# A first block opened by halves of the features, with TensorE kept running from the constants on

## The reference

```
mod = silu(c) @ w_ada + b_ada
shift, scale, gate = split(mod, 3)
h = rms_norm(x, norm_g) * (1 + scale) + shift
proj = h @ w_in            # q, six key and value parts, z_a, branch gates, u, z_s
attn = nsa_attention(...) * silu(z_a)
y = s5_mixer(u, ...)       # a complex linear recurrence over the tokens
ssm = gelu(y) * sigmoid(gelu(y) @ glu_w + glu_b) * silu(z_s)
x = x + gate * (concat(attn, ssm) @ w_out)
```

## Time and profile before

| what | value |
| --- | --- |
| median of 3 runs | 906.59 us (906.15 to 906.69) |
| the profiled execution | 905.98 us, span 904.2 us |
| busy share of the span | TensorE 97%, VectorE 64%, ScalarE 50%, GpSimd 11% |
| chain of waits that ended last, by engine | TensorE 92%, VectorE 4%, ScalarE 2%, transfers 1% |
| mean granted clock of TensorE | 0.997 |

### The profile page before, as it was taken

One profiled execution on the slowest core, in us unless ns is written; L12 is line 12 of the kernel. 1 busy time (PEld: TensorE's weight loads), 2 busy tenths in 40 slices (PEclk: granted clock), 3 DMA queues, 4 the chain that ended last, 5 costly groups with the idle time before them and its releaser, 6 DMA issues.

```text
span 904.2 us, 14652 instructions
## 1 busy us (share of the span) xinstructions
PE 875.7 (97%) x5733; PEld 708.0 (78%) x5733; DVE 578.9 (64%) x1154; ACT 450.7 (50%) x956; POOL 99.7 (11%) x121
## 2 busy tenths in 40 slices
PE   3999999999999999999999999999999999999996
PEld 1579888784677778788888888888888888888885
DVE  5899797989888564666465455345476556445533
ACT  4734323386787334465535466234366554555531
POOL 1001112012400000000010232000000001131202
PEclk9999999999999999999999999999999999999998
DMA  9836655347200313323223424122322332342203
GB/s 384 335 98 140 176 159 168 125 133 240 94 2 2 116 62 118 118 88 95 71 94 116 141 94 131 51 94 94 120 88 67 94 106 96 125 140 71 84 10 94
DMA packets 34678, 104.69 MB, mean 116 GB/s; under 512 B 14961, under 2 KB 14961, under 8 KB 32178
## 3 DMA queue, kind: packets, MB, share of 16 engines
q1 hardware_dynamic: 28098, 85.77, 28.5%
q0 software_dynamic: 3856, 15.73, 5.5%
q10 hardware_dynamic: 2656, 2.26, 1.0%
HBM read 98.37 MB, written 4.19 MB: 113 GB/s over the span
## 4 chain that ended last, share of the span: by engine, by line
PE 92%; DVE 4%; ACT 2%; DMA 1%; issue 1%; SPq 0%; POOL 0%; POOLq 0%; ACTq 0%; DVEq 0%
PE bank L1101 85%; PE bank L1461 2%; PE bank L1615 2%; PE bank L1441 2%; DMA ring<-in_w_ada 1%; PE bank L1501 1%; DVE arena L1749 1%; PE bank L1491 0%; ACT arena L768 0%; DVE xn_t L2271 0%; DVE ring_lo L2295 0%; DVE w_lo L2243 0%; ACT soft L861 0%; DVE pw L1743 0%; DVE x_t L2331 0%
## 5 line engine op out<-in xcount | busy, mean ns | idle before, releaser
L2243 DVE TENSOR_TENSOR w_lo<-ring,w_hi 128x1024 fp32r<-128x1024 f32 x80 | 101.4, 1270 | 51.8 <-ACT w_hi L943 49.3
L1101 PE MATMUL bank<-hT_hi,w_hi 128*128 128x512 f32 x320 | 129.4, 404 | 0.0
L1101 PE MATMUL bank<-hT_lo,w_hi 128*128 128x512 f32 x320 | 125.2, 391 | 0.0
L1101 PE MATMUL bank<-hT_hi,w_lo 128*128 128x512 f32 x320 | 124.9, 390 | 0.0
L1101 PE MATMUL bank<-w_hi,hT_hi 128*128 128x512 f32 x256 | 101.7, 397 | 0.3 <-DVE hT_lo L2289 0.3
L1101 PE MATMUL bank<-w_lo,hT_hi 128*128 128x512 f32 x256 | 99.9, 390 | 0.0
L1101 PE MATMUL bank<-w_hi,hT_lo 128*128 128x512 f32 x256 | 99.8, 390 | 0.0
L943 ACT ACTIVATE w_hi<-ring 128x1024 fp32r<-128x1024 f32 x80 | 84.3, 1057 | 14.0 <-PE bank L1101 13.8
L1101 PEld LDWEIGHTS bank<-hT_hi,w_hi 128*128 128x128 f32 x320 | 60.1, 188 | 16.8 <-issue 4.7
L1101 PEld LDWEIGHTS bank<-hT_lo,w_hi 128*128 128x128 f32 x320 | 60.1, 188 | 13.1
L1101 PEld LDWEIGHTS bank<-hT_hi,w_lo 128*128 128x128 f32 x320 | 60.2, 188 | 11.2
(11 more groups left out here) (341 smaller groups left out, 1834.3 us busy)
## 6 DMA issues: line engine op xcount, KB each, us to landing
ring<-in_w_units SPq DMA_DIRECT2D x80, 512.0 KB, 3.7
ring<-in_w_ada SPq DMA_DIRECT2D x4, 2048.0 KB, 10.3
bias_ring<-in_na_bias POOLq DMA_DIRECT2D x6, 1024.0 KB, 5.2
ring<-in_w_out SPq DMA_DIRECT2D x2, 2048.0 KB, 8.8
bias_ring<-in_t_bias POOLq DMA_DIRECT2D x8, 448.0 KB, 3.7
x_t<-in_x SPq DMA_DIRECT2D x4, 512.0 KB, 5.7
arena<-in_w_ada SPq DMA_DIRECT2D x1, 2048.0 KB, 19.9
arena<-in_w_ada SPq DMA_DIRECT2D x2, 1024.0 KB, 22.8
```

The source lines that it names most:

```text
L1101: return pe.matmul(out, lhsT, rhs, start=first, stop=last)
L2243: dve.tensor_tensor(w_lo[:, u % 4], raw_w[:, u % 4], w_hi[:, u % 4].bitcast(fp32), SUB).then_inc(S["w_split"], 1)
```

## The change

The first block's opening is put in a new order. In words:

- SyncE loads chunk 0 into `arena` and chunk 2 into `cl` (a later part of the arena), then the three parts of the u weights, then chunk 1 into ring slot 1. Chunk 3 follows in two parts into the place of chunk 0, behind a wait for the first product with c; tables, rows and the keys' weights stand behind it.
- TensorE makes five fp32 products of the identity and 512 columns of constants into bank 5, whose result nobody reads, as soon as the constants are there.
- The order of the chunks is 0, 2, 1, 3 (`ADA`): shift and scale of the lower half of the features first. `modulate(0)` waits for chunks 0 and 2 alone, `modulate(1)` for 1 and 3.
- Tile 0 of u is made of three passes as the others are, which adds `part_hi(0)` and `part_lo(0)`. All four tiles are made in two halves of four products a pass (`u_pass`): the lower half of the features, with the last two products with c and their columns among the passes, and then the upper half.
- ScalarE's sines for the tables stand behind the rounding of the upper half; before, ahead of all rounding.
- On VectorE the modulation of the lower half stands ahead of the tables, that of the upper half behind their first operations; `part_lo(12)`, `part_lo(13)` and the lambda products stand behind the keys' squares; before, ahead of them.
- The ring's release for the keys' weights is given once, by two, behind the third product with c and the third tile's first half.

```diff
-            for c, parts in enumerate(chunks):
+            sp.dma_start(arena[:, 0:SLOT], ada[0]).then_inc(ada_late_in[0], 16)
+            sp.dma_start(cl[:, 0:SLOT], ada[2]).then_inc(ada_late_in[1], 16)
+            for c in (CH_U, 1, *range(CH_K, len(chunks))):
+                parts = chunks[c]
...
-                if c >= SLOTS:
+                if c > CH_U:
                     sp.wait_ge(S["w_free"], c - SLOTS + 1)
...
-                if c == SLOTS - 1:
-                    sp.dma_start(arena[:, 0:SLOT], ada[2]).then_inc(ada_late_in[0], 16)
+                if c == 1:
+                    sp.wait_ge(S["ada_done"], 1)
                     for n in range(2):
-                        sp.dma_start(arena[:, SLOT + 2048 * n:SLOT + 2048 * (n + 1)], ada[3][:, 2048 * n:2048 * (n + 1)]).then_inc(ada_late_in[1 + n], 16)
-                elif c == CH_U:
+                        sp.dma_start(arena[:, 2048 * n:2048 * (n + 1)], ada[3][:, 2048 * n:2048 * (n + 1)]).then_inc(ada_late_in[2 + n], 16)
...
+            move_rows(0)
+            move_hT(0)
+            move_hT(1)
+            part_hi(0)
+            move_rows(1)
+            move_hT(2)
+            move_hT(3)
+            round_x(0)
+            part_hi(1)
+            part_hi(2)
+            part_hi(3)
+            move_rows(2)
+            move_rows(3)
+            round_x(1)
+            act.wait_ge(S["ang_ready"], 1)
...
+            def u_pass(f, half, which):
+                w, h = ((p_hi, x_hi), (p_lo, x_hi), (p_hi, hT_r))[which]
...
+                for k in range(4 * half, 4 * half + 4):
+                    if f == 0 and which != 1:
+                        pe.wait_ge(S["h_lower" if which else "h_hi"], k + 1)
+                    ins = mm(bank[f][:, :], w(f)[:, k, :], h[:, k, :], which == 0 and k == 0, which == 2 and k == KD - 1)
...
+            for n in range(5):
+                mm(bank[5][:, :], ident, cons[:, 0:512], True, True)
             pe.wait_ge(S["c_silu"], 1)
...
+            pe.wait_ge(ada_late_in[0], 16)
+            times_c(bank[ROW_PLACE[0]], ada_late[0]).then_inc(S["ada_done"], 1)
+            turn_x(0)
+            mod_columns(0)
+            turn_x(1)
+            pe.wait_ge(ada_late_in[1], 16)
+            times_c(bank[ROW_PLACE[1]], ada_late[1]).then_inc(S["ada_done"], 1)
+            turn_x(2)
+            turn_x(3)
+            mod_columns(1).then_inc(S["mod_cols"], 1)
+            for f, which in ((0, 0), (0, 1), (1, 0), (0, 2), (1, 1), (1, 2)):
+                u_pass(f, 0, which)
+            arrived(1)
+            pe.wait_ge(S["xT_evac"], 2 * NT)
+            times_c(bank[ROW_PLACE[2]], slot(1, KD, 512)).then_inc(S["ada_done"], 1)
+            for which in range(3):
+                u_pass(2, 0, which)
+            pe.wait_ge(S["ada_done"], 3)
+            pe.sem_inc(S["w_free"], 2)
+            for n in range(2):
+                pe.wait_ge(ada_late_in[2 + n], 16)
+                ins = times_c(bank[ROW_PLACE[3]], ada_late[0], range(4 * n, 4 * n + 4))
+            ins.then_inc(S["ada_done"], 1)
+            mod_columns(2)
+            u_pass(3, 0, 0)
+            mod_columns(3).then_inc(S["mod_cols"], 1)
+            u_pass(3, 0, 1)
+            u_pass(3, 0, 2)
+            for f, which in ((0, 0), (0, 1), (1, 0), (1, 1), (0, 2), (1, 2), (2, 0), (2, 1), (2, 2), (3, 0), (3, 1), (3, 2)):
+                u_pass(f, 1, which)
...
+            modulate(0)
+            lower_x(0)
+            part_lo(1)
+            part_lo(2)
+            part_lo(3)
             within(ang)
...
+            modulate(1)
+            lower_x(1)
             settle(dve.memset(pw_r[:, 0, :], 1.0))
...
             squares(keys_w, NG, ss3[:, :, 10:12], qtmp).then_inc(S["k_stats"], 1)
+            part_lo(12)
+            part_lo(13)
```

More of the change, by code:

```diff
@@ L204, in build @@
         mod_rows = soft[:, 0:2 * D]
-        ada_late = [cut(arena[:, n * SLOT:(n + 1) * SLOT], k=KD, n=512) for n in range(2)]
+        ada_late = [cut(v[:, 0:SLOT], k=KD, n=512) for v in (arena, cl)]
+        ADA = [0, 2, 1, 3]
         gate_part = cl[:, 4096:4608]
@@ L278, in build @@
         bias_in = [sem(f"bias_in_{k}") for k in range(2)]
-        ada_late_in = [sem(f"ada_late_in_{k}") for k in range(3)]
+        ada_late_in = [sem(f"ada_late_in_{k}") for k in range(4)]
         u_ahead = [sem(f"u_columns_in_{k}") for k in range(2)]
@@ L669, in _, with move_rows, move_hT @@
             act.activation(th, zr, ACT.Tanh, scale=0.5).then_inc(S["em_ready"], 1)
[L671 to L677, removed]
+            def move_rows(n):
+                act.wait_ge(S["ada_done"], n + 1)
+                act.activation(mod_rows[:, ADA[n] * 512:(ADA[n] + 1) * 512], bank[ROW_PLACE[n]][:, :], ACT.Copy).then_inc(S["mod_row"], 1)
+            def move_hT(i):
                 for b in range(2):
@@ new lines, in u_pass @@
+            def u_pass(f, half, which):
+                w, h = ((p_hi, x_hi), (p_lo, x_hi), (p_hi, hT_r))[which]
+                if not half and which < 2:
+                    pe.wait_ge(S[("p_hi" if f else "u0_hi", "p_lo" if f else "u0_lo")[which]], max(f, 1))
+                for k in range(4 * half, 4 * half + 4):
+                    if f == 0 and which != 1:
+                        pe.wait_ge(S["h_lower" if which else "h_hi"], k + 1)
+                    ins = mm(bank[f][:, :], w(f)[:, k, :], h[:, k, :], which == 0 and k == 0, which == 2 and k == KD - 1)
+                if half and which == 2:
+                    ins.then_inc(S["proj_done"], 1)
@@ L1819, in _, with modulate, lower_x @@
             normal(2)
+            normal(3)
             less_turns(ang, ang2, C2)
-            normal(3)
+            part_lo(0)
             less_turns(ang, ang2, C3)
+            b_ada = col("b_ada")
+            dve.wait_ge(S["xT_evac"], 2 * NT)
+            def modulate(half):
+                dve.wait_ge(S["mod_cols"], half + 1)
+                ks = slice(4 * half, 4 * half + 4)
+                tt(modS[:, ks], bank[4][:, ks], b_ada[:, ks], ADD)
+                stt(modA[:, ks], bank[4][:, KD + 4 * half:KD + 4 * half + 4], 1.0, b_ada[:, KD + 4 * half:KD + 4 * half + 4], ADD, ADD)
+                tt(modA[:, ks], modA[:, ks], col("norm_g")[:, ks], MUL)
+                for k in range(4 * half, 4 * half + 4):
+                    dve.tensor_scalar(hT[:, k, :], hT[:, k, :], modA[:, k:k + 1], modS[:, k:k + 1], MUL, ADD).then_inc(S["h_raw"], 1)
+            def lower_x(half):
+                for k in range(4 * half, 4 * half + 4):
+                    dve.wait_ge(S["h_hi"], k + 1)
+                    dve.tensor_tensor(hT_r[:, k, :], hT[:, k, :], x_hi[:, k, :].bitcast(fp32), SUB).then_inc(S["h_lower"], 1)
+            modulate(0)
[3 more added lines that the diff above has]
+            part_lo(3)
             within(ang)
@@ L1999, in _ @@
             squares(keys_w, NG, ss3[:, :, 10:12], qtmp).then_inc(S["k_stats"], 1)
+            part_lo(12)
+            part_lo(13)
+            for l in range(LAYERS):
+                sl = slice(l * HD, (l + 1) * HD)
+                for m, (a, b) in enumerate((("lq1", "lk1"), ("lq2", "lk2"))):
+                    ins = dve.tensor_tensor_reduce(kc_sb[:, 0:HD], row(a)[:, sl], row(b)[:, sl], 1.0, 0.0, MUL, ADD,
+                                                   lam_t[:, 2 * l + m:2 * l + m + 1])
+                    if 2 * l + m < 2 * LAYERS - 1:
+                        settle(ins)
+            ins.then_inc(S["lam_dot"], 1)
             dve.wait_ge(S["k_rstd"], 1)
```

140 lines of the change are left out of this document (33 added, 107 removed).

## The result

The changed kernel takes 909.37 us (median of 6 runs, 909.06 to 910.02) against 906.47 us (906.04 to 906.69) for the kernel before, run beside it: a ratio of 1.0034, 95% interval 1.0021 to 1.0047. It is slower by 2.9 us, where I had predicted 906.7 us, and the result lies outside my range of 905.6 to 908.6. The profiled execution took 909.88 us around a span of 908.1 us; the span is 3.9 us longer than the 904.2 us of before.

A forecast was written before the change was run, and what follows sets the result against it. TensorE, busy 97% of the span, was taken to bound the kernel. Its 0.7 us gain at the keys would be spent waiting for VectorE's scan, with 0.1 on top: 906.1 profiled, 906.7 on the median's level, range 905.6 to 908.6.

The forecast's parts named there:

- TensorE's gap: Opening, behind the first column products: TensorE idle 1.95 us, from 24.35 to 26.3, until the first modulated tile is rounded.
- ScalarE's pace: First passes over the lower half: four tiles come at 0.55 us each against 0.235 for a product, 0.95 us more, to 28.2.
- the main reason: At the state product: VectorE, 1.6 us late, makes TensorE, 0.7 us early, wait until 130.9; before, 130.75.
- From there TensorE is full: five passes of 0.93 (to 32.85): TensorE's opening from 28.2: five passes at full speed without waiting, followed by a product with c to 34.7.
- rival (1): TensorE's clock falls in the new gap from 21.1 to 26.3: 2.1 us lost makes 908.8 us; chance 0.15.
- The 3.3 us of GpSimd's root are then filled with the moved work: VectorE behind the keys' squares: moved work fills its wait for the root, scaling ends at 104.55 instead of 102.1.
- 130.9 for the state product: Where TensorE takes the states: VectorE's scan starts at 104.6, ends at 130.85, and TensorE waits until 130.9.
- (2): First part of the u weights lands late, 21.65 instead of 20.05; everything shifts by 1.4 us: 908.1; chance 0.1.
- (3): VectorE's chain is a microsecond shorter than summed and TensorE's gain survives: 905.8 us; chance 0.14.
- (4): Five products at the start fail to raise the clock for the first product with c: 1.7 us added, 908.4; chance 0.04.

The follow-up runs named there:

- the gap filled: The changed kernel with two more fp32 products of the identity and constants behind the column products that release the lower half's modulation: 908.43 us, ratio 1.0027.
- the kernel with the parts back: The changed kernel with `part_lo(12)`, `part_lo(13)` and the lambda products put back ahead of the keys' squares: 912.51 us, ratio 1.0065.
- the kernel with the five products alone: The kernel before with only the five fp32 products of constants added at the start, two series: 905.47 us and 905.5 us, ratio 0.9999 in both.
- powers ahead: The changed kernel with the nine operations that make the powers moved ahead of the upper half's modulation on VectorE: 908.32 us, ratio 1.0022.
- scaling late: The changed kernel with VectorE's wait for GpSimd's root and the keys' scaling moved behind the scan, ahead of the keys' use: 907.7 us, ratio 1.0016.

## Why the prediction was wrong

**Right, step by step.** The five products ended at 13.45 (I had 12.9; up to 14.7 in the other profiles), the first product with c took 1.92 us, the transposes started at 16.24 (16.1), TensorE's gap ran from 24.15 to 26.23 (24.35 to 26.3), and ScalarE's pace brought it to 28.23 (28.2). VectorE needed 55.9 us from the first operation of the upper half to the end of the squares (44.00 to 99.87; predicted 42.4 to 98.3, the same length), and 26.25 us for the scan (predicted 26.26). And the main reason held: VectorE, late after the opening, takes back whatever TensorE gains.

**The first step that failed: "From there TensorE is full: five passes of 0.93 (to 32.85)".** Two of them ran at half the clock. That was rival (1), with a chance of 0.15. It came true between its own prices: 1.1 us if the fall hits 28.2 to 30.5, more if it lasts longer; the gap filled gave 1.5, and in the six profiles of kernels with the gap the slow passes end between 30.0 and 31.4. The rival's 908.8 went by 2.1 us; that it lies near the measured 909.4 is luck, since it has too much for the clock and nothing for the root. What was wrong is the chance. I wrote that no row excluded the fall, since the longest wait on TensorE was 0.9 us, and then treated twice that as safe. TensorE had had only transposes and one-column products for 3.3 us before it; whether these count towards the fall no run here separates. The traces do show that waits of 1.8 to 1.9 us behind products of 512 columns left the clock at 1.00 (the wait for `ring_lo`, in four profiles), and that the one of 3.37 us in the kernel with the parts back did not. The Trainium skill (TensorE: Matmul & The Clock Gate, section HAM oscillation — how this bites in real kernels) says that waits between short bursts bring the half rate back and the next burst starts slow. This case's traces agree: the granted clock was 0.54 behind the wait of 2.08 us, with a second pass of 1.6 to 1.9 us in every profile that had the gap, and 0.52 behind the wait of 3.37 us. The example in that section of the Trainium skill has longer waits than the gap here, some 3 to 5 us.

**The second: "The 3.3 us of GpSimd's root are then filled with the moved work".** The filling was costed as if the root kept its time. It took 1.7 us longer beside the moved work, so VectorE waited 1.84 us after it, and the scan started at 107.86. From the end of the squares to the scaling's start it was 5.1 us, not 3.35. No rival of mine had it. The root's rows did not stand among those I used. The pair at 96.01 would have shown only the 3.2 us, but the next pair in the trace of the kernel before shows the slowing itself. GpSimd's timeline and VectorE's, there:

```profile
133.18 1.23 POOL L536 TENSOR_SCALAR small<-small 128x16 f32<-128x16 f32 x1 [33.97 <-DVE small L1963]
134.50 2.90 POOL L537 TENSOR_TENSOR small<-small 128x16 f32<-128x16 f32 x1
```
```profile
133.13 1.22 DVE L1743 TENSOR_TENSOR soft<-arena 128x1024 f32<-128x1024 f32 x1
...
135.64 2.36 DVE L1773 TENSOR_TENSOR ring_lo<-ring,a_hi 128x1024 fp32r<-128x1024 f32 x2
```

The first operation started while VectorE was multiplying SBUF tiles, and took 1.23 us instead of 0.20: it ended 0.06 us after that product. The Trainium skill (SBUF — State Buffer, section Who interferes with whom) has the rule that I should have weighed: a VectorE instruction with two inputs in SBUF contends with a GpSimd instruction that reads SBUF, the lock is exclusive, and the order of issue decides which of the two blocks. The trace of the changed kernel agrees: `part_lo` subtracts one SBUF tile from another, 1.2 us each, and the first of GpSimd's two operations ended at 101.06, when the first `part_lo`, begun at 99.79, was over, instead of after 0.20 us; the second ended 2.8 us after the end of the second `part_lo` (102.14), about its own length alone (2.92). The other order does not agree with that rule, and there the rows decide: two `part_lo` begun at 135.64, in the middle of GpSimd's second operation (134.50 to 137.40), took their usual 2.36 us, and that operation its usual 2.90. So it matters which VectorE operation runs when GpSimd's starts. By these rows VectorE's moved work, started some 0.5 us later, would have left the root at 3.2 us; that is an estimate, and no run tried it.

**The sum.** 130.9 for the state product, 1.5 to 1.6 for the clock and 1.7 for the root make 134.1 to 134.2; measured 134.32. The span grew by another 0.3 us behind that point, which I did not trace. On the medians the loss is 2.9 us, less than the 3.9 us of the two profiled executions, since that of before lay at the low end of its runs and that of the changed kernel near the high end.

**The other rivals.** The u weights were not late (2): ScalarE's rounding started the first pass at 26.23. TensorE's gain did not survive (3). The five products did their work (4).

**What stays open:** why the fall of the clock costs 0.8 us in one execution and 1.6 in another, how much of it is due to the gap's length and how much to the transposes ahead of it, where the clock falls in the rare long runs of the kernel with the five products alone, and why the medians of three experiments (gap filled, powers ahead, scaling late) ended 0.5 to 1.1 us above what was expected.

## What to carry to other kernels

When a reordering trades many small waits for one longer one, price the clock as well as the wait: look at the longest wait that the trace shows without a fall and at what ran ahead of it, and treat anything beyond as undecided, not as free; two products of constants in the gap settled it here. A wait for another engine is only free cover if the work put into it leaves that engine alone; for GpSimd beside VectorE it did not, and 3.2 us of cover were worth 1.5. And where one engine's chain sets the meeting point, time won on the other engine is lost again: taking operations out of VectorE's chain (1.6 and about 2.5 us at the state product, shorter falls of the clock taken off) did as much as filling TensorE's gap (1.5), or more.

## What the runs showed of the hardware

- GpSimd's two operations on 128 x 16 elements took 0.20 and 2.92 us with VectorE idle, and 1.10 and 3.77 us when two subtractions of 128 x 1024 elements had just begun on VectorE, in both kernels. VectorE's subtractions kept their 2.35 us for two. A subtraction that began after GpSimd's operation held up neither (2.90 and 2.36 us, kernel before).
- TensorE's clock fell behind 2.08 us without work that followed 3.3 us of transposes and one-column products, in each of six profiles, and behind 3.37 us that followed products of 512 columns, in the one profile with such a wait. It stayed at 1.00 behind waits of 1.82 to 1.90 us that followed products of 512 columns, in four profiles.
- Products that nobody reads filled the gap (0.26 us of wait left instead of 2.08) and kept the clock up. In the kernel before, with five such products at the start, two runs in twelve were 3.3 to 3.7 us longer than its median, at a mean granted clock of 0.992; the reason was not seen.
